# The three branch gates of sparse attention: computed inside the key/value panels, 268 columns wide, in place of a panel of their own

## What is computed

```python
h = rms_norm(x, norm_mix)
proj = h @ w_in                                  # 1024 x 4748
q_a = proj[..., 0:256]                           # NSA queries, 4 heads of 64
ks_, vs_ = proj[..., 384:448], proj[..., 448:512]   # selected keys, values
kw, vw = proj[..., 512:576], proj[..., 576:640]     # window keys, values
nsa_gates = proj[..., 640:652]                   # 4 heads x 3 branches
...
gates = sigmoid(nsa_gates)
q, ks, kw = rms_norm(q_a), rms_norm(ks_), rms_norm(kw)
o = g[..., 0:1] * o_cmp + g[..., 1:2] * o_sel + g[..., 2:3] * o_win
```

## Time and profile before

| | |
|---|---|
| median of 3 runs | 1525.74 us (1525.13 to 1526.34) |
| the profiled execution | 1524.64 us |
| its span, first to last instruction | 1522.8 us |
| PE busy | 1432.4 us, 94% |
| VectorE, ScalarE, GpSimd busy | 666.2, 356.4, 471.8 us |
| mean granted clock of PE | 0.971 |

### The profile page before, as it was taken

How to read it: one execution, slowest core, us unless ns; L and a number is a source line. 1 busy time by engine, 2 the same in 40 slices (tenths; PEclk the granted TensorE clock), 3 DMA queues, 4 the chain that set the end, 5 groups by cost and what they waited for, 6 DMA issues and landing times.

```text
span 1522.8 us, 18492 instructions
## 1 busy us (share of the span) xinstructions
PE 1432.4 (94%) x7493; PEld 1167.0 (77%) x7493; DVE 666.2 (44%) x1048; ACT 356.4 (23%) x622; POOL 471.8 (31%) x242
## 2 busy tenths in 40 slices
PE   5698799999998899999999979799999999999998
PEld 4588557798887677777778858688888888888887
DVE  5697565534344554444432231532232223354641
ACT  5221444400111133444400020421111111131210
POOL 4324002133534020111033333324343434344542
PEclk9899899999989899999999989999999999999999
DMA  7303101031101000000011031221111111141112
GB/s 177 44 5 64 42 1 29 15 57 53 53 18 35 18 22 15 19 18 18 1 35 53 28 152 49 108 79 42 56 41 55 41 55 41 55 152 56 42 60 106
DMA packets 127862, 76.46 MB, mean 50 GB/s; under 512 B 40352, under 2 KB 114464, under 8 KB 127776
## 3 DMA queue, kind: packets, MB, share of 16 engines
q1 hardware_dynamic: 127792, 75.46, 17.8%
HBM read 66.93 MB, written 8.52 MB: 50 GB/s over the span
## 4 chain that ended last, share of the span: by engine, by line
PE 86%; DVE 8%; ACT 2%; issue 1%; DMA 1%; POOL 0%; SPq 0%; ACTq 0%; DVEq 0%; POOLq 0%
PE ps L634 23%; PE ps L636 22%; PE ps L635 22%; PE ps L1112 3%; PE ps L1142 3%; PE ps L1126 2%; PE ps L867 1%; PE ps L884 1%; PE ps L897 1%; PE ps L649 1%; DVE arena L1496 1%; DMA raw<-in_w_out 1%; DVE hTl L1985 1%; PE ps L1070 1%; PE ps L1089 1%
## 5 line engine op out<-in xcount | busy, mean ns | idle before, releaser
L546 POOL TENSOR_TENSOR wh<-raw,zero 128x1024 fp32r<-128x1024 f32 (+1 forms) x94 | 187.7, 1996 | 1018.3 <-PE ps L636 976.2
L634 PE MATMUL ps<-hTh,wh 128*128 128x512 f32 (+1 forms) x1024 | 408.8, 399 | 3.9 <-ACT arena L1324 3.1
L635 PE MATMUL ps<-hTl,wh 128*128 128x512 f32 (+1 forms) x1024 | 402.2, 393 | 0.0
L636 PE MATMUL ps<-hTh,wl 128*128 128x512 f32 (+1 forms) x1024 | 402.2, 393 | 0.0
L549 POOL TENSOR_TENSOR wl<-raw,wh 128x1024 fp32r<-128x1024 f32 (+1 forms) x94 | 257.9, 2743 | 7.4
L634 PEld LDWEIGHTS ps<-hTh,wh 128*128 128x128 f32 (+1 forms) x1024 | 193.3, 189 | 45.1 <-ACT arena L1324 3.5
L636 PEld LDWEIGHTS ps<-hTh,wl 128*128 128x128 f32 (+1 forms) x1024 | 192.7, 188 | 43.3
L635 PEld LDWEIGHTS ps<-hTl,wh 128*128 128x128 f32 (+1 forms) x1024 | 193.2, 189 | 40.3
L634 PE MATMUL ps<-wh,hTh 128*128 128x512 f32 (+1 forms) x560 | 199.1, 356 | 10.0 <-DVE hTl L1985 6.0
L635 PE MATMUL ps<-wl,hTh 128*128 128x512 f32 (+1 forms) x560 | 198.4, 354 | 0.0
L636 PE MATMUL ps<-wh,hTl 128*128 128x512 f32 (+1 forms) x560 | 198.4, 354 | 0.0
(11 more groups left out here) (324 smaller groups left out, 1513.0 us busy)
## 6 DMA issues: line engine op xcount, KB each, us to landing
raw<-in_w_in SPq DMA_DIRECT2D x37, 512.0 KB, 3.9
raw<-in_w_up SPq DMA_DIRECT2D x32, 512.0 KB, 4.0
raw<-in_w_down SPq DMA_DIRECT2D x16, 512.0 KB, 3.7
merged<-in_x SPq DMA_DIRECT2D x8, 512.0 KB, 7.3
raw<-in_w_out SPq DMA_DIRECT2D x8, 512.0 KB, 3.7
merged<-in_x SPq DMA_DIRECT2D x2, 2048.0 KB, 10.5
x_keep<-merged SPq DMA_DIRECT2D x2, 2048.0 KB, 9.7
conv<-x_keep SPq DMA_DIRECT2D x1, 2048.0 KB, 8.1
```

What stands on the lines that cost most here:

```text
L546: eng.tensor_tensor(wh[:, p, 0:n], raw[:, p, 0:n], zero1[:, 0:1].broadcast_to((P, n)), ALU.add).then_inc(s_hi[0], 1)
L634: mm(out_, ah, bh, start=first, stop=False, skip_group_check=True)
L635: mm(out_, ah, bl, start=False, stop=False, skip_group_check=True)
L636: return mm(out_, al, bh, start=False, stop=last, skip_group_check=True)
```

## The change

The gate panel is dropped from `PANELS`; the two key/value panels become a kind of their own, "kvg", 268 columns wide (`NKV`), so that the twelve gate columns are the last of each token block's product. A block of 268 columns doesn't share a bank with another, so the eight token blocks take eight banks, in the order 4 to 7, 0 to 3 (`KV_ORDER`). VectorE copies 256 columns of each block to `kv_tok` and, after every fourth block, the twelve gate columns of four blocks to `gates`, and raises `kv_read`. ScalarE applies the sigmoid in place on `gates`. The gates' transposes (line 968) and the copy of line 1840 go. Since there is one panel less, the slots of the up and down projections are exchanged (`SWAP`). The number of other panels, products and splits is as it was.

```diff
-           ("row", (OFF_SEL, 0)), ("row", (OFF_SEL, 1)), ("gates", OFF_G)]
+           ("kvg", (OFF_SEL, 0)), ("kvg", (OFF_SEL, 1))]
...
+SWAP = NP % 2
+NKV = 268
+KV_ORDER = (4, 5, 6, 7, 0, 1, 2, 3)
...
-                elif kind == "gates":
-                    eng.dma_start(dst[:, 0:96].rearrange("p (k n) -> p k n", k=KC),
-                                  w_in[0, :, arg:arg + 12].rearrange("(k p) n -> p k n", p=P)).then_inc(landing, 16)
+                elif kind == "kvg":
+                    c0, i = arg
+                    eng.dma_start(dst[:, 0:4 * NKV].rearrange("p (k n) -> p k n", k=4),
+                                  w_in[0, i * 512:(i + 1) * 512, c0:c0 + NKV].rearrange("(k p) n -> p k n", p=P)
+                                  ).then_inc(landing, 16)
...
-            row_panels(p + 3, lambda b: eng.wait_ge(S("main_free"), 19 + b))
-            panel_ready(p + 5)
-            for hf in range(2):
-                eng.wait_ge(S("main_free"), 23 + hf)
-                for kc in range(KC):
-                    w = slice(kc * 12, kc * 12 + 12)
-                    t = slice(hf * HALF, (hf + 1) * HALF)
-                    ins = mm3(ps[0:12, hf, :], wh[:, (p + 5) % 2, w], wl[:, (p + 5) % 2, w],
-                              hTh[:, kc, t], hTl[:, kc, t], kc == 0, kc == KC - 1)
-                ins.then_inc(S("prod"), 1)
+            for i in range(2):
+                panel_ready(p + 3 + i)
+                s = (p + 3 + i) % 2
+                for tb in KV_ORDER:
+                    if i == 0 and tb >= 4:
+                        eng.wait_ge(S("th_done"), 8)
+                        eng.wait_ge(S("br_read"), 8)
+                        eng.wait_ge(S("o_read"), 4)
+                    elif i == 0:
+                        eng.wait_ge(S("main_free"), 19 + tb)
+                    for k in range(4):
+                        kc = 4 * i + k
+                        t = slice(tb * P, (tb + 1) * P)
+                        w = slice(k * NKV, (k + 1) * NKV)
+                        ins = mm3(ps[:, tb, 0:NKV], hTh[:, kc, t], hTl[:, kc, t], wh[:, s, w], wl[:, s, w],
+                                  kc == 0, kc == KC - 1)
+                    if i == 1:
+                        ins.then_inc(S("prod"), 1)
+                if i == 0:
+                    ins.then_inc(S("prod"), 1)
+            eng.wait_ge(S("kv_read"), 1)
...
-            eng.wait_ge(S("gateT"), 2)
-            for tb in range(TB):
-                ins = eng.transpose(ps[:, 0, tb * 12:tb * 12 + 12], gateT[:, tb * P:(tb + 1) * P], ident[0:12, 0:12])
-            ins.then_inc(S("gate_ps"), 1)
...
-            eng.wait_ge(S("prod"), prod_after[P_NSAPROJ + 5])
-            for hf in range(2):
-                eng.activation(gateT[:, hf * HALF:(hf + 1) * HALF], ps[0:12, hf, :], ACT.Sigmoid
-                               ).then_inc(S("gateT"), 1)
+            eng.wait_ge(S("kv_read"), 2)
+            eng.activation(gates[:, :, :].rearrange("p a b -> p (a b)"), gates[:, :, :].rearrange("p a b -> p (a b)"),
+                           ACT.Sigmoid).then_inc(S("gates_ready"), 1)
...
+            for i, tb in enumerate(KV_ORDER):
+                eng.wait_ge(S("prod"), prod_before(P_NSAPROJ + 4) + i + 1)
+                eng.tensor_copy(kv_tok[:, tb, :], ps[:, tb, 0:256])
+                if i % 4 == 3:
+                    t0 = KV_ORDER[i - 3]
+                    eng.tensor_copy(gates[:, t0:t0 + 4, :], ps[:, t0:t0 + 4, 256:NKV]).then_inc(S("kv_read"), 1)
...
-            eng.wait_ge(S("main_free"), 26)
+            eng.wait_ge(S("kv_read"), 2)
...
-            eng.wait_ge(S("gate_ps"), 1)
-            eng.tensor_copy(gates[:, :, :].rearrange("p a b -> p (a b)"), ps[:, 0, 0:96]).then_inc(S("gates_ready"), 1)
```

More of the change, by code:

```diff
@@ L69 @@
 SLOT = 1280
+SWAP = NP % 2
+NKV = 268
+KV_ORDER = (4, 5, 6, 7, 0, 1, 2, 3)
 def merge_panel(q):
     if q < 8:
-        return P_S5MERGE + q if q < 4 else P_NSAPROJ + 6 + q - 4
+        return P_S5MERGE + q if q < 4 else P_NSAPROJ + 5 + q - 4
     return (P_SBMERGE if q < 16 else P_NSAMERGE) + q % 8
@@ L278, in n_prod @@
                 return 1 if arg[1] == 0 else 4
-            if kind == "gates":
-                return 2
+            if kind == "kvg":
+                return 1 if arg[1] == 0 else TB
             if kind == "merge":
@@ L285, in n_elem @@
         def n_elem(kind):
-            return {"col": 1024, "row": 1024, "gates": 96, "merge": 1280, "out": 1024}[kind]
+            return {"col": 1024, "row": 1024, "kvg": 4 * NKV, "merge": 1280, "out": 1024}[kind]
         prod_after, n = [], 0
@@ L477, in load_up @@
             def load_up(j, k):
-                eng.dma_start(raw[:, k, 0:1024].rearrange("p (k n) -> p k n", k=KC),
+                eng.dma_start(raw[:, k ^ SWAP, 0:1024].rearrange("p (k n) -> p k n", k=KC),
                               w_up[0, :, bass.ds(j * P + k * FF, P)].rearrange("(k p) n -> p k n", p=P)
@@ L581, in _ @@
             eng.memset(s5w[:, 4096:6144], 0.0).then_inc(S("toep_zero"), 1)
-            for p in range(3, P_NSAPROJ + 10):
+            for p in range(3, P_NSAPROJ + 9):
                 split_panel(p)
             eng.wait_ge(S("normed"), 1)
-            eng.wait_ge(S("w_split"), P_NSAPROJ + 10)
+            eng.wait_ge(S("w_split"), P_NSAPROJ + 9)
             then(eng.memset(kselT[64:P, :], 0.0))
@@ L610, in _ @@
             eng.wait_ge(S("nsa_consts"), 1)
-            for p in range(P_NSAPROJ + 10, NP):
+            for p in range(P_NSAPROJ + 9, NP):
                 split_panel(p)
@@ L614, in _ @@
                 eng.wait_ge(S("prod"), prod_after[NP - 2 + k])
-                split(k, 1024, S(f"up_in{k}"), 16, (S("up_hi"), k + 1), S("up_split"))
+                split(k ^ SWAP, 1024, S(f"up_in{k}"), 16, (S("up_hi"), k + 1), S("up_split"))
             with eng.Fori(1, 16) as j:
@@ L618, in _ @@
                     eng.wait_ge(S("up_done"), 2 * j + (k - 1))
-                    split(k, 1024, S(f"up_in{k}"), 16 * j + 16, (S("up_hi"), 2 * j + (k + 1)), S("up_split"))
+                    split(k ^ SWAP, 1024, S(f"up_in{k}"), 16 * j + 16, (S("up_hi"), 2 * j + (k + 1)), S("up_split"))
             for d in range(16):
@@ L624, in _ @@
                     dn_consumed(eng, d - 2)
-                split(d % 2, 1024, S(f"dn_in{d % 2}"), 16 * (d // 2 + 1), (S("dn_hi"), d + 1), S("dn_split"))
+                split((d % 2) ^ SWAP, 1024, S(f"dn_in{d % 2}"), 16 * (d // 2 + 1), (S("dn_hi"), d + 1), S("dn_split"))
         @block.tensor
@@ L1586, in evac @@
                 else:
-                    b = (m - 18) % 4
-                    dst = q_tok if m < 22 else kv_tok
-                    ins = eng.tensor_copy(dst[:, 2 * b:2 * b + 2, :].rearrange("p a b -> p (a b)"), ps[:, b, :])
+                    b = m - 18
+                    ins = eng.tensor_copy(q_tok[:, 2 * b:2 * b + 2, :].rearrange("p a b -> p (a b)"), ps[:, b, :])
                 ins.then_inc(S("main_free"), 1)
@@ L1803, in _ @@
                         merge(q, (k - 8,))
-            for m in range(16, 26):
+            for m in range(16, 22):
                 p = P_NSAPROJ
-                evac(m, [prod_before(p) + m - 15, prod_before(p + 2) + m - 17, prod_before(p + 4) + m - 21]
-                     [0 if m < 18 else 1 if m < 22 else 2])
+                evac(m, prod_before(p) + m - 15 if m < 18 else prod_before(p + 2) + m - 17)
                 if m == 17:
```

8 lines of the change are left out of this document (3 added, 5 removed).

## The result

Six runs of the changed kernel have a median of 1517.29 us (1515.15 to 1520.97), six of the kernel before 1526.24 us (1525.13 to 1530.82). The ratio is 0.9937 with a 95% interval of 0.9921 to 0.9953: the change takes 9.6 us off 1526.24, between 7.2 and 12.1 (8.95 us by the medians). The forecast was 1515.9 us and −9.8 us.

What follows compares the result with a forecast made beforehand. PE, busy throughout the stage at full clock, was taken to bound the kernel. The terms −11.11 + 0.97 + 0.1 + 0.2 = −9.8 us, from 1525.74, gave 1515.9 us, range 1513.8 to 1519.5.

Steps and rivals of the forecast that it cites:

- The gate panel, −11.11 us on the path: On PE: 48 matmuls of 231 ns, each making 12 output rows, all on the path; removing them gives −11.11 us.
- Twelve columns, +0.97 us: PE's key/value panels: 192 matmuls become twelve columns wider, 5.0 ns more each by interpolation, +0.97 us.
- Waits ahead of the panels and the eight banks, nothing: Before and behind the key/value panels: banks, splits and copies are ready before PE needs them, so no added time.
- Wait (a), +0.1 us: Before merge 5: PE waits for ScalarE's tanh of merge 4, half 0; +0.1 us, between 0 and 0.4.
- T: PE's end of the key/value panels: 365.07 us in the kernel before, forecast at 366.03 in the changed one.
- Wait (b), +0.2 us: Before merge 5's branch product: PE waits for VectorE's merge 4, behind the normalisation; +0.2 us, between 0 and 1.0.
- Gate transposes, nothing: Before the key transposes: the 8 gate transposes (0.66 us) lie under a wait for VectorE's last merge; removal gains nothing.
- All move up together.: After the stage: key transposes, compression, constants and plan all shift equally, about 9.8 us earlier; nothing waits for a fixed time.
- Rival (3): One PE stretch at the lower clock more or less, 1.7 us: 1514.2 or 1517.6 us; chance 0.05.
- (2): VectorE's chain becomes the bound of merge 5: PE waits 2 to 3 us more, about 1518.4 us; chance 0.10.
- (4): The 268-column matmuls lose the fast pace: +322 ns on each of 192, +62 us, or 1577 us; chance 0.03.
- (5): Between 15 and 58 ns more a matmul eats the gain, about 1523.5 us; chance 0.04.

## Why the prediction was right

**The gate panel, −11.11 us on the path.** Right. Taken out alone it gives 10.93 us in the stage, with 0.18 us of restarts; doubled it costs 11.15 us in the stage and 11 to 12 in the whole. There is no 12-row matmul of 512 columns left.

**Twelve columns, +0.97 us.** The mechanism was right, the size a little high: 4.0 ns a matmul instead of 5.0, 0.76 us. The interpolation was a straight line from 256 to 512 columns; the runs at 268 and 320 show a slope of 0.33 ns over the first twelve, 0.44 up to 320 and 0.42 behind. The bound that I kept for slices that start off the 1024-byte grid wasn't needed. I had named these starts wrongly, as odd multiples of 48 bytes: the slices start at multiples of 1072 bytes, 0, 48, 96 and 144 bytes off that grid.

**Waits ahead of the panels and the eight banks, nothing.** Right: 51.60 us with eight banks, 51.56 with four.

**Wait (a), +0.1 us.** Right. The tanh of merge 4, half 0 starts at 377.07 and is followed by the second half; PE resumes with merge 5 at 377.79, T + 13.66 where it wanted T + 13.64, and with 0.31 us between its first two starts.

**Wait (b), +0.2 us.** The chain was right to a tenth: the query passes were forecast to end at T + 23.9, and T + 23.9 is 388.0, where the merge starts. The loss was smaller, 0.06 us in the restart, for PE had come 0.1 us later itself. The order of turns between VectorE and GpSimd was as played through: line 1841 free, line 1844 free, then alternating; what differs is that VectorE's pass of line 1845 shows 4.41 us and GpSimd's first 2.95, each holding part of its wait for the other. The 2.83 us that the sum takes for GpSimd's second pass stands in none of its rows; undisturbed ones take 2.94 and 2.89 us (at 392.46 and 406.06 in the kernel before), 0.1 us that the sum doesn't feel.

**Gate transposes, nothing.** Right: PE now idles 0.94 us where it idled 0.35 us and worked 0.66 before. The sum over the stage: −11.11 + 0.76 + 0.21 (from merge 4 to the key transposes, 28.55 against 28.34 us) = −10.14 us, where −9.8 was forecast.

**"All move up together."** This is the step that holds only on average. The stage is fixed to a hundredth of a microsecond between two profiles; what follows it isn't. The key transposes come 11.8 us earlier (1.7 of it from ahead of the panels), the end only 6.1. That the shift shrinks later in the plan was named as a sign of being wrong, by a wait that isn't relative; PE's idle time behind the stage fell by 3.0 us, so it is the clock and no wait. Rival (3) had one low-clock stretch more or less, ±1.7 us, at a chance of 0.05. (Its price was read with the count of the weight loads, 9; the row has 10 matmuls. Measured at its place a stretch costs about 1.5 us.) In the first profile of the changed kernel it was several: with a mean clock of 0.967 against 0.971, what is missing to full clock over the span is 1516.7 × 0.033 = 50.1 us against 1522.8 × 0.029 = 44.2 us, 5.9 us more. PE's busy time fell by only 3.9 us (1432.4 to 1428.5) and not by the 11 us of the stage, its idle time by 2.2. And the clock's share isn't a draw alone: it changes with where the rest of the kernel lies in time, of which the stretch behind the compression is the part that the runs show. That the medians came out near the sum owes something to luck: kernels whose stage is only 0.8 us shorter are 5 us faster, and one with a useless 0.9 us is 4.2 us slower. The changed kernel's median lies 1.4 us above the forecast and 2.2 us inside the range; three of its six runs stand within 0.8 us of 1515.9, and one, 1520.97, outside the range.

Rivals (2), (4) and (5) are out: the wait for VectorE's chain costs 0.06 us, and a 268-column matmul takes 124 ns.

## What to carry to other kernels

Columns that lie next to a panel already streamed cost their own width (0.76 us here), a panel of their own costs full streams, however few rows they make (11.1 us for 12 rows). When a piece of PE work is taken out, write down what had been lying under it on the other engines and play their turns through against the new times; here the cover was gone to the last tenth of a microsecond, and still held. And when two kernels differ by 1% or less, look at the granted clock of each before crediting the difference to the work: move the rest of the kernel by a few useless matmuls and see whether the difference stays.

## What the runs showed of the hardware

- Streams of 268 float32 columns, whose slices start off the 1024-byte grid, keep the pace of the others: 120.0, 124.0, 146.7 and 227.3 ns for 256, 268, 320 and 512 columns.
- A matmul of this kind costs the same with few output rows: 231 ns with 12 rows and 227 ns with 128, at 512 streamed columns.
- A low-clock stretch behind sparse PE work is a matter of place: the same 8.1 to 8.2 us of compression, at full clock, was followed by a stretch at 0.50 when it started 189.3 to 190.0 us behind an earlier low stretch, and by none at 188.6 to 188.8 or 191.6. These are eight single profiles. One stretch costs about 1.5 us at its place, but the kernels with and without it differ by 4 to 5 us in the whole, or by 0.4, or, for the kernel before, by 2 us the other way. What decides the later stretches stays open.
- Some instructions of VectorE wait for the whole of a GpSimd split pass, and the pass for them: a TENSOR_SCALAR of 32 elements took 1.76 us beside a pass and 0.18 us without one, and the split pass of line 553 took 4.88 us beside the query passes where an undisturbed one takes 2.94. Others don't: a TENSOR_REDUCE of 1024 elements (at 368.75 us in the kernel before) took 1.22 us in the midst of a split pass, no more than its half of the 2.29 us of 2048 elements without one.
